# Moving a decode selection into the attention tasks, and cached window keys into the projections, in a one-core hybrid decoder step

## The chip, the cores and the metric

The kernel runs on one NeuronCore of one Trainium2 chip. The metric is device microseconds (us) of one execution, from a median of several runs. Everything is float32. The engines are PE (TensorE; PEld is its weight load), DVE (VectorE), ACT (ScalarE), POOL (GpSimd) and SP (SyncE, which here only starts DMAs). Each engine runs its own list of instructions in order, and semaphores tie the lists together.

## The reference

One layer is applied to a prompt (1 x 512 rows of width 1024) and to a decode group (8 sequences, one new row each, 2048 cached rows in 16 pages each). The part that the change touches is the attention of the decode group:

```python
def nsa_attend(q, gates, qpos, kc, vc, ks, vs, kw, vw, kw_pos):
    s = einsum('bqghd,bngd->bqghn', q, kc) * scale            # compressed branch, 127 blocks
    p = masked_softmax(s, ...)
    o_cmp = einsum('bqghn,bngd->bqghd', p, vc)
    imp = p.sum(axis=3)                                       # importance, summed over the 4 heads of a group
    # score of 33 selection blocks from imp; the first and the last two are forced
    ...
    _, idx = lax.top_k(score, 16)                             # selected branch: 16 of 33 blocks of 64 keys
    s = einsum('bqghd,bqgksd->bqghks', q, k_g) * scale
    o_slc = einsum(..., masked_softmax(s, mask), v_g)
    s = einsum('bqghd,bwgd->bqghw', q, kw) * scale            # window branch: last 512 rows (cached state)
    o_win = einsum('bqghw,bwgd->bqghd', masked_softmax(s, wmask), vw)
    g = sigmoid(gates)
    return g[..., 0:1] * o_cmp + g[..., 1:2] * o_slc + g[..., 2:3] * o_win
```

Around it stand a projection `h @ w_in` (queries, keys and values of three branches, gates, an S5 input), a compression of keys and values by two small layers, an S5 recurrence, a gated merge and an MLP of width 4096. There are 16 heads in 4 groups, the head dimension is 64.

## The kernel before

The whole layer is one program whose order is written out by hand. In time it falls into these stages:

- **Projections** (0 to 302 us). `UNITS` lists them; PE runs one after the other (`projection(u, unit)`), and each writes one of two pairs of PSUM banks (0 to 3), which ACT empties. A "gemm" unit is 16 matmuls of 128 x 260 (L1870); `("tr", c, m)` transposes the tile of keys or values just made; `("y", ii)` are outputs of the S5 recurrence, `("h0",)` and `("st",)` its state in and out. `ENDS_BEHIND` places the four `chunk_ends(ii)` (L1979), that feed the recurrence on DVE, behind units.
- **Key units inside the projections.** The scores of the decode queries against the 2048 cached keys of the selected branch are taken straight from the raw pages. One of 16 units k holds 8 pages of one sequence: SP loads four of them (L706) and POOL gathers four (L872) into one of seven buffers `KL`; DVE transposes the buffer in 32 x 32 blocks into one of two `KT` (L1452); and PE runs 32 matmuls of 32 x 32 by 256 (`key_scores`, L1996) into banks 4 to 7. `KEYS_BEHIND` tells behind which projection unit they stand, some singly and some in twos. Buffer k < 4 is its own, then three go round; `wait_key_buffer` says when one may be filled.
- **Compression** (302 to 453 us). Pages of the compressed cache come through a ring of three slabs (`PLAN`, `SLAB`), DVE permutes them (L1500), PE runs layer 1 (L2041) and layer 2 (L2050, L2052). Scores of the prompt's compressed branch run in between (`compressed_scores`, `compressed_probs` on DVE).
- **Decode selection** (453 to 496 us). Products of the decode queries with the compressed keys (L2071) and the gates (L2073); softmax; importance (L2137); top 16 of 33 by comparing all pairs on 32 partitions (L1612 to L1617); the chosen blocks as a mask added to the 2048 scores `SA` (L1585, L1588), softmax. In the same stage the window branch is scored: `key_t(r)` transposes the cached window keys of one half sequence by four PE transposes, ACT copies them to `XT` (L1103), `key_s` multiplies (L2123); 16 such steps from two slabs `("winrows", (0, bh))`. `head_probs(v)` then transposes ten groups of probabilities (0 to 3 prompt, 4 to 7 selected, 8 window, 9 the rest), in L2091 or L1847, and ACT copies them out (L1144).
- **Attention tasks** (496 to 661 us). 48 tasks `TASKS[n]`, software pipelined: at n, PE runs `scores(n)` (L2153), `probs(n-2)` (transposes, L1847) and `values(n-3)` (L2185, L2190); DVE adds the causal mask (L1657), takes the maximum (L1659), then scales and copies for the tasks before; ACT takes exponentials (L1166). Twelve `decode_values` steps (L2204 to L2215) multiply the decode probabilities with values, at the tasks in `V_AT`: 1, 5, 9, ... 45.
- **Merge and MLP** (661 us to the end), bound by PE (L2277).

Of the kernel before, what the change touches and what calls it, by code (L numbers as in the profile page):

```python
# [6 lines left out]
ALU = mybir.AluOpType  # L7
# [6 lines left out]
P = 128  # L14
# [49 lines left out]
CO_HSUMT = CO_HSUM + 32  # L64
CO_BM = CO_HSUMT + P
# [7 lines left out]
CO_HSUMT2 = CO_PERM + P  # L73
CO_PERMT = CO_HSUMT2 + P
CO_BM2 = CO_PERMT + P
CO_ALL = CO_BM2 + NB


def shape_constants():
# [9 lines left out]
    c[:, CO_HSUM:CO_HSUM + 32] = i[:, None] // HPG == np.arange(32)[None, :]  # L89
    c[:32, CO_HSUMT:CO_HSUMT + P] = i[None, :] // HPG == np.arange(32)[:, None]  # L90
    c[:, CO_BM:CO_BM + NB] = i[:, None] // NH == np.arange(NB)[None, :]
# [8 lines left out]
    c[:32, CO_HSUMT2:CO_HSUMT2 + P] = (NG * (i // HPG % NB) + i // 32)[None, :] == np.arange(32)[:, None]  # L100
    c[:, CO_BM2:CO_BM2 + NB] = i[:, None] // HPG % NB == np.arange(NB)[None, :]
    j = np.arange(NSEL)
    tie = np.broadcast_to((j[None, :] < j[:, None]).astype(np.float32), (32, NSEL, NSEL)).copy()
    return c, tie
# [9 lines left out]
def stream_plan():  # L114
# [9 lines left out]
    plan += [("winrows", (0, bh), 4, 0) for bh in range(2)]  # L124
# [26 lines left out]
def projection_units():  # L151
# [8 lines left out]
            ("y", 2), q_units[2], q_units[3], ("y", 3), ("st",)]  # L160
    prev = None
    for c in range(3):
        for m in range(4):
            rest.append(("gemm", ("win", (C_KV + KVW * c, 512)), m, P, ("kv", c, m)))
            if prev is not None:
                rest.append(("tr", *prev))
            prev = (c, m)
# [10 lines left out]
def label(unit):  # L178
# [12 lines left out]
KEYS_BEHIND = {("kv", 0, 1): (0, 1), ("tr", 0, 1): (2,), ("tr", 0, 2): (3,), ("tr", 0, 3): (4, 5), ("tr", 1, 0): (6,),  # L191
               ("tr", 1, 1): (7,), ("tr", 1, 2): (8, 9), ("tr", 1, 3): (10,), ("tr", 2, 0): (11,),
               ("tr", 2, 1): (12, 13), ("tr", 2, 2): (14,), ("tr", 2, 3): (15,)}
# [3 lines left out]
def build(nc, a):  # L197
    with ExitStack() as ctx:
# [119 lines left out]
        sw_read = sem("sw_read")  # L318
# [4 lines left out]
        xt_full = sem("xt_full")  # L323
        xt_ready = sem("xt_ready")
        xt_used = sem("xt_used")
# [14 lines left out]
        s_full = sem("s_full")  # L340
# [95 lines left out]
        XT = QO[:, 6224:8272].rearrange("p (s c) -> p s c", s=4)  # L436
# [7 lines left out]
        kcT = R[:, 5216:5216 + 8 * 2 * (NC + 2)].rearrange("p (b q n) -> p b q n", b=8, q=2)  # L444
# [3 lines left out]
        SA = QO[:, 4160:6209]  # L448
        SAT = SA[:, 0:2048].rearrange("p (x a t) -> p a x t", a=4, t=32)
        SW = R[:, 13921:14434]  # L450
        SC = R[:, 14434:14563]
        IMP = R[0:32, 14564:14697]
        SSEL = R[0:32, 14700:14733]
        SELX = R[:, 14740:14773]
        GDN = R[:, 14774:14776]
        CMPB = R[0:32, 9824:10913].rearrange("p (j i) -> p j i", j=NSEL)
        CMPA = R[0:32, 10913:12002].rearrange("p (j i) -> p j i", j=NSEL)
        MORE = R[:, 12002:12002 + CO_ALL - CO_N]
        PERM, HSUMT2, PERMT = (MORE[:, c - CO_N:c - CO_N + P] for c in (CO_PERM, CO_HSUMT2, CO_PERMT))
        BM2 = MORE[:, CO_BM2 - CO_N:CO_ALL - CO_N]  # L460
        TIE = R[0:32, 12400:13489].rearrange("p (j i) -> p j i", j=NSEL)
        GH = R[:, 13500:13548]
# [12 lines left out]
        PCF = [R[:, c:c + 512].rearrange("p (h n) -> p h n", n=32) for c in (15968, 16796, 17308, 3072)]  # L475
# [92 lines left out]
        def key_buffer(k):  # L568
            return k if k < 4 else 4 + (k - 4) % 3

        def key_count(k):
            return 64 if k < 4 else 64 * ((k - 4) // 3 + 1)
# [4 lines left out]
        def wait_key_buffer(eng, k):  # L577
# [1798 lines left out]
```

## Time and profile before

| what | value |
|---|---|
| median of 3 runs | 1363.39 us (1362.45 to 1364.57) |
| the profiled execution | 1360.91 us, its span 1359.1 us |
| PE busy | 1251.5 us (92%) |
| DVE busy | 828.9 us (61%) |
| ACT, POOL busy | 305.1 us (22%), 355.7 us (26%) |
| 453.1 to 497.2 us | PE busy 28.4 of 44.1 us, granted clock 0.82 |
| 497.2 to 661 us | PE busy 155.4 and DVE 129.6 of 163.8 us, granted clock 1.00 |

The span runs from the first to the last instruction on the chip; the execution's own time is 1.8 us more. The stretches are read from the view that adds up busy time by window, the rest from the page.

### The profile page before, as it was taken

How to read it: one execution, taken by the hardware profiler on the slowest of the kernel's cores; microseconds unless marked ns; L12 is line 12 of the kernel's file. 1: busy time of each engine (PE TensorE's matmuls, PEld its weight loads, DVE VectorE, ACT ScalarE, POOL GpSimd, SP SyncE). 2: the span in 40 equal slices, each digit the busy share in tenths (PEclk: the TensorE clock that was granted, in tenths of full speed). 3: DMA queues.
4: the chain of work that ended last, by engine and by line, in shares of the span. 5: the costliest groups of instructions: out<-in, count | busy, mean ns of one | idle time of the engine just before them, and what ended most of it. 6: DMA issues, size and time to landing. Idle time of an engine off the chain costs nothing.

```text
span 1359.1 us, 20576 instructions
## 1 busy us (share of the span) xinstructions
PE 1251.5 (92%) x7761; PEld 1017.1 (75%) x7761; DVE 828.9 (61%) x1370; ACT 305.1 (22%) x831; POOL 355.7 (26%) x422
## 2 busy tenths in 40 slices
PE   6889899999999669999999999986999999999995
PEld 5778776668887445565788888775888888888885
DVE  7779332227888477777766554657565465466445
ACT  3463311120010355565410111032000000000012
POOL 5942324312220012222111111110111112513542
PEclk9899899899999889999999999996999999999998
DMA  9223445547667333535561332330122132131101
GB/s 264 72 79 121 148 108 170 160 146 257 242 248 248 105 91 106 162 97 167 178 225 63 109 92 80 140 111 29 62 97 90 63 114 72 62 124 63 63 1 63
DMA packets 122002, 166.15 MB, mean 122 GB/s; under 512 B 36448, under 2 KB 90400, under 8 KB 117552
## 3 DMA queue, kind: packets, MB, share of 16 engines
q1 hardware_dynamic: 103408, 104.72, 24.8%
q0 software_dynamic: 8080, 50.58, 10.5%
q10 hardware_dynamic: 10416, 9.54, 2.1%
q8 instruction: 62, 1.02, 0.3%
q14 instruction: 36, 0.29, 0.1%
HBM read 159.34 MB, written 13.84 MB: 127 GB/s over the span
## 4 chain that ended last, share of the span: by engine, by line
PE 81%; DVE 12%; issue 3%; ACT 3%; POOL 0%; DMA 0%; DVEq 0%; ACTq 0%; PEldq 0%
PE PS L2277 44%; PE PS L1870 13%; PE PS L2041 8%; PE PS L1847 4%; PE PS L1996 2%; PE PS L2185 2%; PE PS L2153 2%; DVE small L1659 2%; PE PS L2215 1%; DVE PS L1657 1%; DVE R L1677 1%; PE PS L1979 1%; PE PS L2020 1%; DVE hT L1259 1%; PE PS L2190 1%
## 5 line engine op out<-in xcount | busy, mean ns | idle before, releaser
L1870 PE MATMUL PS<-hT,stream 128*128 128x260 f32 (+1 forms) x800 | 187.7, 395 | 6.5 <-ACT KVU L1061 4.1
L1870 PEld LDWEIGHTS PS<-hT,stream 128*128 128x128 f32 (+1 forms) x800 | 153.7, 194 | 38.4 <-issue 6.0
L2277 PE MATMUL PS<-R,stream 128*128 128x260 f32 x720 | 168.9, 383 | 2.4 <-PE PS L2277 2.4
L2277 PEld LDWEIGHTS PS<-R,stream 128*128 128x128 f32 x720 | 135.7, 190 | 25.8 <-issue 5.5
L2277 PE MATMUL PS<-R 128*128 128x260 f32 x576 | 134.3, 390 | 3.3 <-DVE R L1822 2.1
L2277 PEld LDWEIGHTS PS<-R 128*128 128x128 f32 x576 | 111.7, 194 | 22.1 <-DVE R L1822 2.5
L2041 PE MATMUL PS<-R 128*128 128x256 f32 (+1 forms) x544 | 121.9, 383 | 5.2 <-DVE R L1500 2.4
L2277 PE MATMUL PS<-R,QO 128*128 128x260 f32 x544 | 123.6, 383 | 1.4 <-DVE QO L1703 1.4
L1777 DVE TENSOR_TENSOR R<-PS,R 128x260 f32<-128x260 f32 x100 | 42.6, 426 | 129.5 <-PE PS L2277 128.8
L2041 PEld LDWEIGHTS PS<-R 128*128 128x128 f32 x544 | 102.1, 197 | 22.1 <-issue 6.1
L2277 PEld LDWEIGHTS PS<-R,QO 128*128 128x128 f32 x544 | 103.3, 190 | 17.6 <-DVE QO L1703 1.8
L1777 DVE TENSOR_TENSOR KVU<-PS,KVU 128x260 f32<-128x260 f32 x92 | 39.1, 426 | 101.3 <-PE PS L2277 90.8
L2277 PE MATMUL PS<-hT,stream 128*128 128x260 f32 x384 | 94.8, 390 | 3.7 <-PE PS L2277 3.0
L1500 DVE STREAM_TRANSPOSE R<-stream 128x2048 f32<-128x2048 f32 (+1 forms) x34 | 75.2, 2233 | 20.5 <-PE PS L1996 9.8
L2277 PEld LDWEIGHTS PS<-hT,stream 128*128 128x128 f32 x384 | 73.1, 193 | 18.7 <-issue 6.8
L1452 DVE STREAM_TRANSPOSE R<-R 128x2048 f32<-128x2048 f32 x14 | 32.0, 2302 | 86.7 <-PE PS L1996 86.1
L872 POOL DMA_INDIRECT R<-in_cache_kv_slc,row_kv x56 | 53.4, 953 | 117.3 <-DVE R L1452 53.2
L1211 ACT ACTIVATE R<-PS 128x260 f32<-128x260 f32 x56 | 21.5, 386 | 273.9 <-PE PS L2277 273.9
L645 POOL TENSOR_SCALAR R<-R,small 128x512 f32<-128x512 f32 (+3 forms) x64 | 48.1, 755 | 132.8 <-DVE small L1664 132.8
L1847 PEld LDWEIGHTS PS<-consts,R 128*128 128x128 f32 (+1 forms) x424 | 47.6, 145 | 41.5 <-issue 34.1
L1847 PE MATMUL PS<-consts,R 128*128 128x128 f32 (+1 forms) x424 | 61.2, 286 | 13.3 <-DVE R L1677 6.2
L1166 ACT ACTIVATE R<-PS,small 128x512 f32<-128x512 f32 (+3 forms) x128 | 65.9, 525 | 10.9 <-DVE small L1659 10.0
(420 smaller groups left out, 1931.2 us busy)
## 6 DMA issues: line engine op xcount, KB each, us to landing
stream<-in_cache_kv_slc SPq DMA_DIRECT2D x128, 128.0 KB
stream<-in_w_mlp_up SPq DMA_DIRECT2D x8, 2048.0 KB
stream<-in_w_mlp_down SPq DMA_DIRECT2D x8, 2048.0 KB
stream<-in_w_in SPq DMA_DIRECT2D x4, 2048.0 KB
stream<-in_state_kv_win SPq DMA_DIRECT2D x16, 512.0 KB
stream<-in_w_in SPq DMA_DIRECT2D x8, 1024.0 KB
out_kv_win_sample<-in_state_kv_win POOLq DMA_DIRECT2D x1, 8176.0 KB, 43.3
R<-in_cache_kv_slc SPq DMA_DIRECT2D x56, 128.0 KB
```

The costliest lines, as they stand in the source:

```text
L645: return eng.tensor_scalar(S, S, ainv[:, k:k + 1], gtm[:, t, col:col + 1], ALU.mult, ALU.mult)
L872: pool.indirect_dma_start(key_pages(k)[:, x, :], None, slc_rows, bass.IndirectOffsetOnAxis(ap=row_kv[:, at:at + 1], axis=0)).then_inc(keys ...
L1166: ins = nc.scalar.activation(PP[:, n % 2, j, c0:c0 + P * (t + 1)], score_block(n, j, c0), ACT.Exp, bias=amx[:, k:k + 1], accum_out=asm[:, ...
L1452: V.transpose(KT[k % 2], KL[key_buffer(k)]).then_inc(kt_ready, 1)
L1500: V.transpose(ROWST[:, w % 3, 0:256 * ns].rearrange("p (s x) -> p s x", x=256), slab(s)[:, 0:512 * ns].rearrange("p (s k x) -> p k s x", k ...
L1659: V.reduce_max(amx[:, k:k + 2 * nx], S[:, :, 0:P * (t + 1)], AX, negate=True).then_inc(as_max, 1)
L1777: V.tensor_tensor(to, product_of(w, i), other, ALU.add).then_inc(pr_added, 1)
L1847: return nc.tensor.transpose(out, in_, ident[0:rows, 0:rows])
L1870: ins = M(pair(u)[0:w, hf, 0:HALF], lhs[k], rhs[k][:, HALF * hf:HALF * hf + HALF], start=(k == 0), stop=(k == n - 1))
L1996: ins = M(PS[32 * g:32 * g + 32, 4 + a4, cols], QM[rows, 256 * b + c0:256 * b + c0 + 32], keys[rows, :, c0:c0 + 32], start=(k == 0 and dh ...
L2041: ins = M(out, w1c[:, kind, x, :], rhs, start=(x == 0), stop=(x == 7))
L2277: ins = M(product_of(w, i), lhs[:, k, :], rhs[:, k, :], start=(k == 0), stop=(k == nk - 1))
```

## The change

- **The window keys become four key units** of the projections (`NWU = 4`, two sequences each, 64 matmuls of 32 x 32 by 128), ahead of the sixteen page units. Their scores `SW` are copied out once by ACT behind `("tr", 0, 2)`. `key_t`, `key_s`, `XT` and the two `("winrows", (0, bh))` slabs go.
- **One key unit at a time**: ten stand between the two halves of a gemm unit (`KEYS_INSIDE`), ten behind a transpose unit (`KEYS_BEHIND`). Page loads use buffers 2 to 6 in turn at first, then 4 to 6. SP takes pages 0 to 3 of a unit and POOL 4 to 7 (before: even and odd ones), SP reads four page numbers by one load, and the compression weights come in four parts between page loads.
- **Two units move**: `("st",)` from behind `("y", 3)` to behind the first gemm unit of keys; `chunk_ends(0)` from behind `("h0",)` to behind `("q", 7)`.
- **The selection moves into the tasks**: DVE's steps stand behind tasks 0 to 9 (`selection(n)`), PE's behind 1 and 4 (`selection_products(n)`), and groups 8, 4, 5, 6, 7, 9 of the probabilities behind 8, 10, 11, 12, 13, 14 (`PROBS_AT`), all through bank 4. The pair comparison runs on 128 partitions over 297 elements, not on 32 over 1089. Only groups 0 to 3 stand ahead of the tasks. The `decode_values` steps stand at 15, 16, 18, 21, 24, 27, 30, 31, 33, 36, 40, 44.
- The gates' product (L2073) moves into the compression stage, and one `compressed_probs` of two moves from step 6 to step 5.

```diff
-ENDS_BEHIND = [("h0",), ("q", 4), ("y", 0), ("y", 1)]
+ENDS_BEHIND = [("q", 7), ("q", 4), ("y", 0), ("y", 1)]
...
-NKU = 2 * NB
-KEYS_BEHIND = {("kv", 0, 1): (0, 1), ("tr", 0, 1): (2,), ("tr", 0, 2): (3,), ("tr", 0, 3): (4, 5), ("tr", 1, 0): (6,),
...
+NWU = NB // 2
+NKU = NWU + 2 * NB
+KEYS_INSIDE = {("kv", 0, 1): 0, ("kv", 0, 2): 2, ("kv", 1, 0): 4, ("kv", 1, 1): 6, ("kv", 1, 2): 8, ("kv", 1, 3): 10,
+               ("kv", 2, 0): 12, ("kv", 2, 1): 14, ("kv", 2, 2): 16, ("kv", 2, 3): 18}
+KEYS_BEHIND = {("tr", 0, 0): 1, ("tr", 0, 1): 3, ("tr", 0, 3): 5, ("tr", 1, 0): 7, ("tr", 1, 1): 9, ("tr", 1, 2): 11,
+               ("tr", 1, 3): 13, ("tr", 2, 0): 15, ("tr", 2, 1): 17, ("tr", 2, 2): 19}
+KEY_BUFFER = [0, 1, 2, 3, 4, 5, 6, 2, 3] + [4 + k % 3 for k in range(NKU - 9)]
...
+            elif k < 12:
+                eng.wait_ge(kt_ready, (3, 4, 5, 6, 7)[k - 7])
             else:
                 eng.wait_ge(kt_ready, k - 2)
...
-        PT_BANK = (0, 1, 2, 3, 5, 6, 7, 5, 6, 7)
+        PT_BANK = (5, 6, 7, 5, 4, 4, 4, 4, 4, 4)
...
+        N_PC, N_IMP, N_SEL, N_SELX, N_MASK, N_SWE, N_SAE, N_SWP, N_SAP = 0, 1, 3, 4, 5, 6, 8, 7, 9
+        PROBS_AT = {8: 8, 10: 4, 11: 5, 12: 6, 13: 7, 14: 9}
+        PT_ORDER = [0, 1, 2, 3] + list(PROBS_AT.values())
...
-        V_AT = {1 + 4 * i: step for i, step in enumerate(V_STEPS)}
+        V_AT = dict(zip((15, 16, 18, 21, 24, 27, 30, 31, 33, 36, 40, 44), V_STEPS))
...
-                        key_loads(4, 5, 6)
-                        compression_weights()
-                        key_loads(7, 8, 9)
+                        key_loads(*range(4, 12))
+                        sp.wait_ge(kt_ready, 9)
+                        for q in range(3):
+                            compression_weights(q)
+                            key_loads(12 + q)
...
+            def selection(n):
+                if n == N_PC:
+                    dve.wait_ge(sc_exp, 1)
...
+                if n == N_SEL:
+                    Si = SSEL.unsqueeze(1).to_broadcast([P, JQ, NSEL])
+                    Sj = SJ[:, 0].unsqueeze(2).to_broadcast([P, JQ, NSEL])
...
+                if n == N_MASK + 1:
+                    selected(0)
+                    selected(1)
+                if n == N_MASK + 2:
+                    selected(2)
+                    selected(3)
+                    V.reduce_max(dmx[:, 1:2], pmx, AX, negate=True).then_inc(samax, 1)
+                if n == N_SWP:
+                    dve.wait_ge(sexp, 1)
...
+                if n == N_SAP:
+                    dve.wait_ge(saexp, 1)
...
+            pe.wait_ge(pcp_ready, TT)
+            for v in range(4):
+                head_probs(v)
+            scores(0)
             pe.wait_ge(pt_ready, 4)
-            scores(0)
-            pe.wait_ge(pa_ready, 1)
-            for v in range(4, 8):
-                head_probs(v)
-            pe.wait_ge(p_ready, 1)
-            head_probs(8)
-            head_probs(9)
-            pe.wait_ge(pt_ready, 10)
             for n in range(NTK + 3):
...
+                selection_products(n)
+                if n in PROBS_AT:
+                    head_probs(PROBS_AT[n])
+                if n == min(V_AT):
+                    pe.wait_ge(pt_ready, 10)
                 if n in V_AT:
                     decode_values(*V_AT[n])
```

In the program's order the change looks as follows. First PE in the projections, before, behind the last S5 output unit: `L1847 ... small` is the unit `st`, L1870 a gemm unit, L1996 a key unit.

```order
L1847 MATMUL PS<-consts,small 128x128 [waits h_ready,hs_ready,pair_free]
L1847 MATMUL PS<-consts,small 16x128
L1847 MATMUL PS<-consts,small 128x128
L1847 MATMUL PS<-consts,small 16x128
L1870 MATMUL PS<-hT,stream 128x260 [waits slab_in0,pair_free]
L1870 MATMUL PS<-hT,stream 128x260 x15
L1870 MATMUL PS<-hT,stream 128x260 [waits slab_in0,pair_free]
L1870 MATMUL PS<-hT,stream 128x260 x15
L1996 MATMUL PS<-R 32x256 [waits kt_ready,ends_free,qm_ready]
L1996 MATMUL PS<-R 32x256 x31
L1996 MATMUL PS<-R 32x256 [waits kt_ready]
L1996 MATMUL PS<-R 32x256 x31
```

The same place after (L1886 was L1847, L1911 was L1870, L2042 is a window key unit):

```order
L1911 MATMUL PS<-hT,stream 128x260 [waits slab_in0,pair_free]
L1911 MATMUL PS<-hT,stream 128x260 x15
L1886 MATMUL PS<-consts,small 128x128 [waits h_ready,hs_ready,pair_free]
L1886 MATMUL PS<-consts,small 16x128
L1886 MATMUL PS<-consts,small 128x128
L1886 MATMUL PS<-consts,small 16x128
L1911 MATMUL PS<-hT,stream 128x260 [waits slab_in0,pair_free]
L1911 MATMUL PS<-hT,stream 128x260 x7
L2042 MATMUL PS<-R 32x128 [waits kt_ready,ends_free,qm_ready]
L2042 MATMUL PS<-R 32x128 x63
L1911 MATMUL PS<-hT,stream 128x260 x8
L1886 MATMUL PS<-consts,QO 128x128 [waits pair_free]
```

The unit `st` stands between two gemm units instead of ahead of them, and a window unit of 64 matmuls splits the second one.

Then PE between the products with the compressed keys (L2071) and the first tasks, before. The list starts at the decode masks' products; the window key steps stand ahead of it:

```order
L2153 MATMUL PS<-KVU,QO 128x512 [waits pt_ready]
L2153 MATMUL PS<-KVU,QO 128x512
L2091 MATMUL PS<-R,QO 128x128 [waits pt_ready,pa_ready]
L2091 MATMUL PS<-R,QO 128x128 x3
L2091 MATMUL PS<-R,QO 128x128 [waits pt_ready]
L2091 MATMUL PS<-R,QO 128x128 x3
L2091 MATMUL PS<-R,QO 128x128 [waits pt_ready]
L2091 MATMUL PS<-R,QO 128x128 x3
L2091 MATMUL PS<-R,QO 128x128 [waits pt_ready]
L2091 MATMUL PS<-R,QO 128x128 x3
L1847 MATMUL PS<-consts,R 128x128 [waits pt_ready,p_ready]
L1847 MATMUL PS<-consts,R 128x128 x3
```

After, from the products with the compressed keys (L2124) on; L2173 is `scores`, L2159 the importance, L2205 and L2210 `values`:

```order
L2124 MATMUL PS<-QO,R 32x129 [waits l2_ready,qpad_ready]
L2124 MATMUL PS<-QO,R 32x129 x15
L1886 MATMUL PS<-consts,QO 128x128 [waits pcp_ready]
L1886 MATMUL PS<-consts,QO 128x128 x11
L1886 MATMUL PS<-consts,QO 128x128 [waits pt_ready]
L1886 MATMUL PS<-consts,QO 128x128 x3
L2173 MATMUL PS<-KVU,QO 128x512 x2
L2173 MATMUL PS<-KVU,QO 128x512 [waits pt_ready]
L2173 MATMUL PS<-KVU,QO 128x512
L2159 MATMUL PS<-R,consts 128x127 [waits pc_ready]
L2173 MATMUL PS<-KVU,QO 128x128 [waits as_exp]
L2173 MATMUL PS<-KVU,QO 128x128 x3
```

Between these products and `scores(1)` only the prompt's sixteen transposes are left; the sixteen matmuls of L2091 with their wait on `pa_ready` are gone from here.

Last DVE in the tasks 2 to 4 after (L1695 mask and L1697 maximum begin a task, L1715 ends its own work); before, nothing stood between an L1677 copy and the next mask:

```order
L1715 COPY R<-PS 128x512 [waits at_full]
L1640 TENSOR_TENSOR R<-R 128x297 [waits tie_in]
L1641 TENSOR_TENSOR R<-R 128x297
L1642 TENSOR_TENSOR R<-R 128x297 [waits dve_ch]
L1643 TENSOR_TENSOR R<-R 128x297 [waits dve_ch]
L1644 TENSOR_REDUCE R<-R 128x9 [waits dve_ch]
L1647 TENSOR_SCALAR R<-R 32x9 [waits dve_ch]
L1647 TENSOR_SCALAR R<-R 32x9 x2
L1647 TENSOR_SCALAR R<-R 32x6
L1695 TENSOR_TENSOR PS<-PS,consts 128x2x128 [waits as_full]
L1697 TENSOR_REDUCE small<-PS 128x2 [waits as_mask]
```

The comparison of pairs now stands between the copy of one task and the mask of the next.

## Rows read from the trace of the kernel before

**Rows 1.** The page: instruction fetches among the DMA queues; the chain's shares

```profile
q8 instruction: 62, 1.02, 0.3%
...
PE 81%; DVE 12%; issue 3%; ACT 3%; POOL 0%; DMA 0%; DVEq 0%; ACTq 0%; PEldq 0%
```

**Rows 2.** Chain of waits, 450 to 498 us: start, length, engine, tile, line

```profile
453.14 0.59 PE PS L2073 x2
...
478.24 0.70 DVE QO L1585
...
484.22 2.10 ACT QO L1135 x2
...
486.74 1.30 DVE QO L1634
...
488.54 5.83 PE PS L2091 x32
...
497.22 0.44 DVE PS L1657
```

**Rows 3.** Timeline, 450 to 500 us: start, length, engine, line, operation [idle before]

```profile
456.12 1.28 ACT L1130 ACT_TABLE_LOAD   x1
...
461.12 1.28 DVE L1612 TENSOR_TENSOR R<-R 32x1089 f32<-32x1089 f32 x1
...
488.39 0.16 DVE L1639 RECIPROCAL small<-small 128x1 f32<-128x1 f32 x1
...
490.57 1.22 DVE L1659 TENSOR_REDUCE small<-PS 128x2 f32<-128x1024 f32 x1
490.65 0.60 ACT L1144 ACTIVATE R<-PS 128x512 f32<-128x512 f32 x1 [3.64 <-PE PS L2091]
```

**Rows 4.** Windows of the tasks: PE, PEld, DVE, ACT, POOL busy, clock, DMA

```profile
497.22:526.98 29.76, 27.37 (x293) 17.00 (x287) 23.97 (x48) 18.27 (x64) 9.02 (x12) 1.00 0.25 72
526.98:543.62 16.64, 16.14 (x164) 10.33 (x164) 13.35 (x26) 9.34 (x30) 5.02 (x6) 1.00 0.41 120
543.62:661.00 117.38, 111.83 (x1150) 71.41 (x1152) 92.32 (x184) 69.68 (x232) 34.73 (x48) 1.00 0.47 141
```

**Rows 5.** Timeline of PE in the tasks

```profile
509.73 1.92 PE L2215 MATMUL PS<-stream,R 128*16 128x256 f32 x32
...
518.49 1.09 PE L1847 MATMUL PS<-consts,R 128*128 128x128 f32 x8
```

**Rows 6.** Timeline of PE in the projections

```profile
156.54 16.79 PE L1870 MATMUL PS<-hT,stream 128*128 128x260 f32 x64 [4.13 <-ACT KVU L1061]
173.25 2.76 PE L1996 MATMUL PS<-R 32*32 32x256 f32 x128
...
176.55 7.18 PE L1870 MATMUL PS<-hT,stream 128*128 128x260 f32 x32
...
213.67 0.73 PE L1996 MATMUL PS<-R 32*32 32x256 f32 x26
...
220.07 8.74 PE L1870 MATMUL PS<-hT,stream 128*128 128x260 f32 x32
...
249.26 0.69 PE L1996 MATMUL PS<-R 32*32 32x256 f32 x26
...
255.66 9.71 PE L1870 MATMUL PS<-hT,stream 128*128 128x260 f32 x32
```

**Rows 7.** Windows in the projections, the columns as in rows 4

```profile
157.00:162.00 5.00, 5.00 (x14) 3.88 (x14) 3.25 (x2) 0.25 (x2) 3.79 (x4) 0.54 0.86 269
```

**Rows 8.** Timeline of PE around the first chunk ends

```profile
80.04 3.59 PE L1979 MATMUL PS<-QO,R 128*128 128x136 f32 x16 [3.72 <-issue]
```

**Rows 9.** Timeline of ACT in the same stretch

```profile
79.63 0.60 ACT L1010 ACTIVATE QO<-PS 128x520 f32<-128x520 f32 x1
```

**Rows 10.** Timeline of POOL: one gather of a page

```profile
224.11 0.95 POOL L872 DMA_INDIRECT R<-in_cache_kv_slc,row_kv  x1 [0.30 <-issue]
```

**Rows 11.** Timeline of PE in the compression stage

```profile
428.43 7.17 PE L2041 MATMUL PS<-R 128*128 128x256 f32 x32 [2.36 <-DVE R L1500]
```

More of the change, by code:

```diff
@@ L166, in projection_units @@
                 rest.append(("tr", *prev))
+            if prev is None:
+                rest.append(("st",))
             prev = (c, m)
@@ L568, in key_buffer, with key_landed @@
         def key_buffer(k):
-            return k if k < 4 else 4 + (k - 4) % 3
-        def key_count(k):
-            return 64 if k < 4 else 64 * ((k - 4) // 3 + 1)
+            return KEY_BUFFER[k]
+        def key_landed(k, windows, pages):
+            mine = [i for i in range(k + 1) if KEY_BUFFER[i] == KEY_BUFFER[k]]
+            return 16 * sum(windows if i < NWU else pages for i in mine)
         def key_pages(k):
@@ L1031, in _ @@
                     nkv += 1
+                    if (c, m) == (0, 2):
+                        act.wait_ge(k_done, NWU)
+                        for a4 in range(4):
+                            ins = nc.scalar.activation(SWT[:, a4], PS[:, 4 + a4, 0:P].rearrange("p (x t) -> p x t", t=32),
+                                                       ACT.Copy)
+                        ins.then_inc(sw_ready, 1)
                     continue
@@ L1863, in open_pair, with gemm @@
                     pe.wait_ge(pair_free, u - 1)
-            def gemm(u, lhs, rhs, w=P):
+            def gemm(u, lhs, rhs, w=P, inside=None):
                 n = len(lhs)
                 for hf in range(2):
+                    if hf == 1 and inside is not None:
+                        key_scores(inside)
                     for k in range(n):
@@ L1905, in projection @@
                     S = slab(n)[:, 0:KD * width].rearrange("p (k c) -> p k c", c=width)
-                    ins = gemm(u, [S[:, k, P * m:P * m + w] for k in range(KD)], [hT[:, k, :] for k in range(KD)], w)
+                    ins = gemm(u, [S[:, k, P * m:P * m + w] for k in range(KD)], [hT[:, k, :] for k in range(KD)], w,
+                               KEYS_INSIDE.get(unit[4]))
                     ins.then_inc(pair_full, 1)
@@ L2014, in compressed_products @@
                     pe.wait_ge(sa_ready, 1)
+                    M(PS[:, 4, 136:184], consts[0:NB, CO_BMT:CO_BMT + P], gs8[0:NB, :], start=True,
+                      stop=True).then_inc(gates_full, 1)
                 else:
@@ L2116, in key_s @@
-            def key_s(r0):
-                pe.wait_ge(xt_ready, r0 + 4)
-                if r0 == 0:
-                    pe.wait_ge(sc_max, 1)
-                for r in range(r0, r0 + 4):
-                    b, p = KR[r]
-                    jj, bh = b // 2, b % 2
-                    M(PS[32 * jj:32 * jj + 32, 4, :], QP[:, p, b, :], XT[:, r % 4, :],
-                      start=(bh == 0 and p == 0), stop=(bh == 1 and p == 1)).then_inc(xt_used, 1)
-                if r0 == 12:
-                    pe.wait_ge(xt_used, 16)
-                    pe.sem_inc(s_full, 1)
@@ L2129, in _, with selection_products @@
-            for r in range(len(KR) + 1):
-                if r < len(KR):
-                    key_t(r)
-                if r % 4 == 1 and r >= 5 or r == len(KR):
-                    key_s((r - 1) // 4 * 4 - (4 if r < len(KR) else 0))
-                if r == R_IMP:
+            def selection_products(n):
+                if n == N_IMP:
                     pe.wait_ge(pc_ready, 1)
-                    M(PS[0:32, 5, 0:NC], consts[:, CO_HSUM:CO_HSUM + 32], SC[:, 0:NC], start=True,
+                    M(PS[:, 4, 192:192 + NC], consts[:, CO_HSUM:CO_HSUM + P], SC[:, 0:NC], start=True,
```

381 lines of the change are left out of this document (187 added, 194 removed).

## The prediction

> **What bounds the kernel now.** I read the chain of waits first: PE holds 81% of it and DVE 12% [rows 1], so a microsecond counts where PE's list waits, not where an engine merely has work. Then I walked the chain through the decode selection. The products with the compressed keys end at 453.14 [rows 2], and the first mask of the steady tasks starts at 497.22 [rows 2]. In between the chain runs over DVE masks and maxima, one exponential of 2049 columns on ACT, a scaling, and transposes [rows 2]: 44.1 us of serial steps with PE used in part only.
>
> The tasks behind it are different. By the windows, PE is busy for 27.37 of the first 29.76 us, DVE for 23.97 [rows 4]; over the rest PE for 111.83 of 117.38 and DVE for 92.32 [rows 4]. PE sets the pace, DVE has a fifth to spare. Added DVE work is therefore half hidden there, added PE work hardly.
>
> In the projections PE runs matmul after matmul, with three disturbances. PE waits 4.13 us for ACT, and the two gemm units behind it take 16.79 us [rows 6] where one takes 7.18 [rows 6]; the granted clock over those 5 us is 0.54 [rows 7], a mean between the two levels (1.2 and 2.4 GHz), after an idle stretch. And two key units stop in their middle: they start at 213.67 and 249.26 and are followed by the next gemm unit at 220.07 and 255.66 [rows 6]; the gemm units behind take 8.74 and 9.71 us. In both stops PE waits for nothing that the profile names.
>
> **Ahead of the tasks.** What goes: the whole way from 453.14 to 497.22, 44.1 us. What stays, from the same start: two small DVE steps of about 0.3 each (between the 0.16 of one element and the 0.70 of 512 columns [rows 2, 3]), 0.6; the table load 1.28 [rows 3] and a 127-column exponential, 0.5; the first copy 0.60 [rows 3], since the fourth group of transposes shares its bank; that group's four transposes and `scores(0)`, 1.09 each [rows 5]; mask and maximum of task 0, 0.44 + 1.22 [rows 2, 3]; the first step of the selection, 0.65. Sum 7.5, and the mask of task 1 starts there. Gain 44.1 - 7.5 = **-36.6**.
>
> **Inside the tasks, DVE.** The selection's DVE steps do not vanish; now they queue between one task's copy and the next task's mask, and PE's `scores` and `values` wait behind. By rows: eight 512-column steps (four mask adds, four maxima) at 0.72, the 0.70 [rows 2] and a gap, 5.8 and the window's maximum 0.7; the scaling of 2049 columns 1.30 [rows 2]; the window's scaling 0.5; the comparison, five steps of 297 elements. One of 1089 took 1.28 [rows 3]; on a line from 0.16 for one element that is 0.47, so 2.35 instead of 6.4. Some thirty small steps at 0.16 to 0.3 [rows 3] make 4.5. Total 15.2, of which 14.5 lies in tasks 1 to 9. Before, that stretch lasted 29.76 with 23.97 on DVE [rows 4]; after, DVE alone needs 23.97 + 14.5 = 38.5, and I take 39.3 with its semaphore steps: +9.5. PE's small products (importance, mask, window group) then lie under DVE.
>
> **Inside the tasks, PE.** Groups 4 to 7 and 9 of the probabilities stand behind tasks 10 to 14: four at 1.09 [rows 5] and 0.6, 5.0 on the engine that paces. Before, that stretch held PE for 16.14 of 16.64 [rows 4] with one value step of 1.92 [rows 5], now moved later. 16.1 - 1.9 + 5.0 = 19.2; about 0.5 of waits: +3. Here the wait for `pa_ready` (DVE, behind task 9) holds `scores(11)`, and DVE has 2.9 us of its own work meanwhile, so I add 1 for all such handovers. The value steps: four more fall behind task 15, where PE paces (an `own` step of 1.5 and three of 1.92 [rows 5]): 7.3, of which the 5.5 idle us of PE there [rows 4] may take a little: +6.5. Tasks together **+20** (15 to 28).
>
> **Projections.** (1) `st` behind the first key gemm: ACT empties the last S5 unit while PE multiplies. The wait 4.13 goes, and the slow gemms with it: 16.79 - 2 x 7.18 = 2.43 [rows 6]; a new wait of 0.3 for the first key tile's copy. -6.3. (2) `chunk_ends(0)` behind `q 7`: PE was idle 3.72 us before it [rows 8]. But `q 7` needs the bank pair of `q 6`, and ACT empties that only at 79.63 + 0.60 [rows 9], behind its chunk copies. The idle time stays; DVE gets its input some 4 us later and had over 10 to spare. 0 (to -1.9). (3) Four window units. Two page units (128 records of 32 x 256) took 2.76 [rows 6]. A window unit has 128 records of half the columns. If the issue of instructions sets the rate, it costs 2.76; if the columns do, 1.38. A 32 x 256 record at sixteen at once would be far below the 22 ns that each took, so issue is nearer: +11.0 (5.5 to 11.0). The sixteen page units cost what they did.
>
> The Trainium skill, TensorEngine Tiling (Array Packing), section Key Properties, says that different tiles load weights and multiply in parallel; by that alone the columns would count, and the sum would be 5.5 lower. No row has a 32 x 128 form.
>
> (4) The two stops. From start to the next gemm 6.40 each time [rows 6] where a unit takes 1.4, so 5.0 each, and 1.56 + 2.53 in the slow gemms behind: 14.1 in all. Both came in the first unit behind two in a row, with page loads under way. In the new order no two stand together, but a window unit is as many instructions as two page units, and more bytes move early. I keep 8 of the 14.1: -6 (-14 to +14). Projections together **-1.3**.
>
> The Trainium skill, Runtime: NRT & Kernel Launch, section Instruction fetch mechanics, says that instructions come in 16 KiB blocks and that this is mostly hidden. The block size agrees with 62 packets for 1.02 MB [rows 1]; that it is hidden doesn't agree with the stops, if they are fetches, which no row proves.
>
> **Compression.** PE waited 2.36 us for a DVE transpose [rows 11] behind the two `compressed_probs` in one step; spread, that goes. The gates' product, 0.59 [rows 2], is now there. **-1.8** (-2.4 to 0). SP loads two slabs fewer.
>
> **Sum.** -36.6 + 20 - 1.3 - 1.8 = -19.7. The profiled execution took 1360.9 us, so 1341.2; the median is 2.5 higher, 1363.4, and by it **1344**.
>
> **Rivals.** *More is gained*: the stops go altogether (-8 more) and a window unit costs its columns (-5.5): 1344 - 13.5 = 1330. For it: no two units together. Against: the record rate of [rows 6].
>
> *The chain moves into the tasks*: DVE's steps of one task become the wait of PE, whose wait delays the next mask, and PE, idle for 3 us at a time, falls to the lower clock as at [rows 7]. Price: PE's work in tasks 1 to 9, 27.4, at a mean clock of 0.75 (estimated between 0.54 [rows 7] and 1), +9, and 3 of handovers: 1356. Against it: DVE never waits for a result younger than one task.
>
> *Slower, PE stops in the projections*: window units fetch as many instructions in 2.76 us as the pairs did, and five page buffers plus the window rows keep the queues full. A stop costs 14.1 / 2 = 7 us. The forecast holds about one; it takes 19.7 / 7, three more, to eat the gain, so it decides from the fourth. With six, 1344 + 35 = 1379. For it: both stops of before; against: fourteen other units passed.
>
> *The pages come too late*, so the fixed order buys nothing: POOL's gather takes 0.95 + 0.30 [rows 10], four a unit are 5.0 us, and PE asks for a unit each (7.18 + 0.7 + 2.8) / 2 = 5.3. Covered by 0.3 only. At 6.3 a unit, eleven units behind the five buffers wait 1 us each: 1355.
>
> **How the numbers follow.** The forecast has 0.66, with its own range 1334 to 1354 from the bounds above; more gained 0.13; chain in the tasks 0.10; pages late 0.04; slower 0.07. The range takes in the first rival's edge and the middle ones: 1331 to 1359. A measurement of this kernel tells 0.2%, about 2.7 us, from no change. Faster by more: all but the last case and a tail, 0.90; within 0.03; slower 0.07.
>
> **What would show it.** Right: the mask of task 1 about 8 us behind the end of the products with the compressed keys; DVE over 90% busy in tasks 1 to 9; each task with a probability group about 1 us longer; window units of 2.8 us; no wait for ACT ahead of the second key gemm; a granted clock near 1 from the products to the last task. Wrong: PE waits without a named cause in more than two key units; PE waits for `kt_ready`; a clock under 0.9 in the tasks; value steps that wait for DMA, since SP now has them closer together.

## The result, and the profile after

The changed kernel took **1383.9 us** (median of 4 runs, 1383.3 to 1389.0) beside 1362.9 (4 runs, 1357.8 to 1364.6) for the kernel before: a ratio of 1.0176 with a 95% interval of 1.0156 to 1.0196. It is slower by 21 us where 19 us faster was forecast. That is the case with the chance 0.07, the rival "PE stops in the projections".

The chain of waits of the changed kernel, at its landmarks (start us, length us, what). The rows answer to [rows 2] and [rows 6].

```profile
152.05 7.01 PE PS L1911 x32
...
348.81 3.31 PE PS L2094 x14
...
494.61 1.95 PE PS L2124 x32
...
503.01 0.44 DVE PS L1695
...
687.47 2.61 PE PS L1911 x11
```

They are the first key gemm, the start of the compression, the end of the products with the compressed keys (at 496.56), the mask of task 1 and the gemm behind the tasks. Beside those of before, stage by stage:

| stage | before | after | difference | forecast |
|---|---|---|---|---|
| start to the compression | 302.5 | 348.8 | +46.3 | -1.3 |
| compression to the end of its products | 150.7 | 147.8 | -2.9 | -1.8 |
| products to the mask of task 1 | 44.1 | 6.4 | -37.6 | -36.6 |
| tasks, from that mask to the next gemm | 164.1 | 184.5 | +20.4 | +20 |
| the rest | 697.8 | 694.0 | -3.8 | 0 |
| span | 1359.1 | 1381.5 | +22.4 | -19.7 |

Four stages came within 4 us of what was forecast. One did not, and it outweighs them. What happened in it stands on the chain, here from the first window unit on:

```profile
164.60 0.38 PE PS L2042 x16
164.98 0.15 issue
165.13 0.26 PE PS L2042
165.39 1.86 issue
167.25 0.26 PE PS L2042
167.51 1.18 issue
168.69 0.37 PE PS L2042
169.05 1.03 issue
170.09 2.67 PE PS L2042 x105
172.76 4.56 PE PS L1911 x16
```

"issue" is time in which PE waits for nothing that the profile names. The trace holds two records for each matmul, so a window unit has 128 records and a page unit 64. PE runs 16 records, then one at a time, 0.4 to 2.1 us from one to the next, then the others without a pause, 25 ns each. The half gemm behind takes 4.56 us instead of 3.7, with a granted clock of 0.81 over it. The same is seen, to more or less of it, in twelve more units. The next lines are page unit 5, which stops, and units 6 and 7, which do not:

```profile
221.22 1.24 PE PS L2047 x41
...
222.53 0.38 PE PS L2047
222.91 1.04 issue
223.95 0.62 PE PS L2047 x3
224.57 0.81 issue
225.38 1.12 PE PS L2047 x18
226.50 4.99 PE PS L1911 x16
231.49 1.43 PE PS L2047 x60
...
237.16 1.43 PE PS L2047 x60
```

POOL's own row of instructions (start us, us) says what else went on at 221 to 224. Behind 223.45 its next gather is at 241.31:

```profile
219.69 0.95 POOL L887 DMA_INDIRECT R<-in_cache_kv_slc,row_kv  x1 [8.39 <-DVE R L1465]
...
223.45 0.95 POOL L887 DMA_INDIRECT R<-in_cache_kv_slc,row_kv  x1 [0.30 <-issue]
241.31 0.95 POOL L887 DMA_INDIRECT R<-in_cache_kv_slc,row_kv  x1 [16.91 <-DVE R L1465]
```

Units 4, 6, 7 and 16 to 18 ran clean; these are the units beside which no page load is under way. Unit 19 stands beside two gathers of the compression (333.05 and 334.30) and took 3.1 us, with two short pauses, where unit 18 took 1.5. But SP's loads, POOL's gathers and DVE's transposes all come together, each started by the transpose of an earlier unit. The trace alone can't tell which of them stops PE, or whether so many short instructions in a row do it by themselves. One thing it does tell. Over the stop of the first window unit, 164.90 to 170.10 us, the queues moved this (packets, MB, share of 16 engines):

```profile
q0 software_dynamic: 197, 0.52, 37.2%
q10 hardware_dynamic: 176, 0.15, 8.3%
q1 hardware_dynamic: 83, 0.07, 5.5%
```

No packet of instructions is among them, and none in the stops at 262.80 to 265.90 and 281.30 to 284.40 either. So what ends these three is not the arrival of a block of instructions.

### The profile page after: what moved, and what is told of

Its sections match the earlier page's. It is cut to its first block, busy times and chain, and to the rows that moved or that the text cites. A ratio compares the mean times of both kernels' runs of the same rounds, so it can differ in the third digit from the quotient of the medians.

```text
span 1381.5 us, 21274 instructions
## 1 busy us (share of the span) xinstructions
PE 1276.5 (92%) x8182; PEld 1027.1 (74%) x8182; DVE 835.8 (61%) x1382; ACT 297.0 (22%) x819; POOL 355.4 (26%) x422
## 3 DMA queue, kind: packets, MB, share of 16 engines
q8 instruction: 65, 1.06, 0.3%
## 4 chain that ended last, share of the span: by engine, by line
PE 84%; DVE 9%; issue 4%; ACT 2%; POOL 0%; DMA 0%; DVEq 0%; ACTq 0%; PEldq 0%; POOLq 0%
PE PS L2298 43%; PE PS L1911 15%; PE PS L2094 8%; PE PS L1886 4%; PE PS L2047 3%; PE PS L2173 2%; PE PS L2205 2%; DVE small L1697 1%; PE PS L2235 1%; PE PS L2042 1%; PE PS L1976 1%; DVE PS L1695 1%; DVE R L1514 1%; DVE R L1715 1%; PE PS L2073 1%
## 5 line engine op out<-in xcount | busy, mean ns | idle before, releaser
L1911 PE MATMUL PS<-hT,stream 128*128 128x260 f32 (+1 forms) x800 | 201.2, 412 | 6.8 <-ACT QO L1026 4.0
L1911 PEld LDWEIGHTS PS<-hT,stream 128*128 128x128 f32 (+1 forms) x800 | 159.7, 203 | 45.7 <-issue 10.5
L2298 PEld LDWEIGHTS PS<-R,stream 128*128 128x128 f32 x720 | 135.7, 190 | 25.8 <-issue 5.5
L2298 PE MATMUL PS<-R 128*128 128x260 f32 x576 | 130.8, 383 | 3.3 <-DVE R L1861 2.1
L2298 PEld LDWEIGHTS PS<-R 128*128 128x128 f32 x576 | 109.3, 190 | 21.1 <-DVE R L1861 2.5
L2094 PEld LDWEIGHTS PS<-R 128*128 128x128 f32 x544 | 100.8, 194 | 20.2 <-issue 5.4
L1465 DVE STREAM_TRANSPOSE R<-R 128x2048 f32<-128x2048 f32 x18 | 41.6, 2311 | 122.1 <-PE PS L2047 85.4
L887 POOL DMA_INDIRECT R<-in_cache_kv_slc,row_kv x64 | 60.9, 952 | 175.9 <-DVE R L1465 82.2
L1886 PEld LDWEIGHTS PS<-consts,R 128*128 128x128 f32 (+1 forms) x403 | 45.8, 146 | 40.5 <-issue 35.0
L1886 PE MATMUL PS<-consts,R 128*128 128x128 f32 (+1 forms) x403 | 59.1, 289 | 13.2 <-POOL R L650 6.9
```

The lines of the kernel that those rows point to most:

```text
L887: pool.indirect_dma_start(key_pages(k)[:, x, :], None, slc_rows, bass.IndirectOffsetOnAxis(ap=row_kv[:, at:at + 1], axis=0)).then_inc(keys ...
L1465: V.transpose(KT[k % 2], KL[key_buffer(k)]).then_inc(kt_ready, 1)
L1886: return nc.tensor.transpose(out, in_, ident[0:rows, 0:rows])
L1911: ins = M(pair(u)[0:w, hf, 0:HALF], lhs[k], rhs[k][:, HALF * hf:HALF * hf + HALF], start=(k == 0), stop=(k == n - 1))
L2094: ins = M(out, w1c[:, kind, x, :], rhs, start=(x == 0), stop=(x == 7))
L2298: ins = M(product_of(w, i), lhs[:, k, :], rhs[:, k, :], start=(k == 0), stop=(k == nk - 1))
```

## Experiments

Every experiment has runs of the kernel before beside it, on the same chip: e1 to e4 on chip A, e5 and e7 to e9 on B, e10 to e13 on C, e14 and e16 to e18 on D, e15 and e19 on C again. The chip of the result above is not known, and no experiment ran the changed kernel as it is on A or B.

**Which loads.** Three kernels leave out page loads behind unit 6. PE's instructions stay the same.

```diff
-            for k in range(NWU, NKU):
+            for k in range(NWU, 7):
                 wait_key_buffer(pool, k)
...
-                for k in units:
+                for k in [k for k in units if k < 7]:
                     wait_key_buffer(sp, k)
```

The first piece alone is e2, the second alone e3, both are e1. DVE's waits count accordingly.

> The changed kernel without the page loads of key units 7 to 19, SP's and POOL's both; these units multiply what lies in their buffers. PE's instructions, their order and the transposes stay. Theory (page traffic): PE's stops inside key units come from the page loads that are under way; without them units 7 to 19 take 2.8 to 3.2 us each, PE's time from 151.9 to the compression falls from 197 to about 160, and the time from 1384 to about 1347. Rival (instructions): the units' own 256 instructions cannot be supplied at this rate whatever the queues do; then the stops stay, and the time is 1384 less at most 5.

> The changed kernel without POOL's half of the page loads (the gathers) of units 7 to 19; SP's half stays. If POOL's gathers are what stops PE, the time is about 1347, as without any page load. If any traffic does it, in proportion, about half of the gain: 1365. If SP's loads do it, 1384.

> The changed kernel without SP's half of the page loads of units 7 to 19; POOL's gathers stay. If POOL's gathers are what stops PE, about 1384; in proportion to traffic 1365; if SP's loads do it, 1347.

Measured, with the kernel before at 1359.8: e1 1336.4 (2 runs), e2 **1336.9** (2 runs), e3 **1382.2** (2 runs, 1379.7 to 1384.7). Where 1347 was expected, 10 us less came; which theory holds doesn't hang on that. Beside the 1383.9 of the result, SP's half costs nothing that two runs can tell, and POOL's half costs all of it. The groups of PE between 150 and 350 us (busy, mean ns, idle time before them), first of the changed kernel, then of e2, then of e3:

```profile
L1911 PE MATMUL PS<-hT,stream 128*128 128x260 f32 (+1 forms) x416 | 110.5, 426 | 1.3 <-issue 1.3
L2047 PE MATMUL PS<-R 32*32 32x256 f32 x1024 | 41.6, 395 | 10.4 <-issue 9.2
L2042 PE MATMUL PS<-R 32*32 32x128 f32 x512 | 14.4, 350 | 9.1 <-issue 8.9
```

```profile
L1913 PE MATMUL PS<-hT,stream 128*128 128x260 f32 (+1 forms) x416 | 98.3, 391 | 0.3 <-issue 0.3
L2049 PE MATMUL PS<-R 32*32 32x256 f32 x1024 | 25.3, 385 | 0.5 <-DVE R L1467 0.4
L2044 PE MATMUL PS<-R 32*32 32x128 f32 x512 | 10.4, 306 | 4.4 <-issue 4.4
```

```profile
L2049 PE MATMUL PS<-R 32*32 32x256 f32 x1024 | 43.3, 387 | 7.2 <-issue 5.6
L2044 PE MATMUL PS<-R 32*32 32x128 f32 x512 | 15.1, 339 | 8.8 <-issue 8.7
```

The page units fell from 52.0 us with their idle time to 25.8, and the gemms from 110.5 to 98.3, though SP kept loading. Over 164 to 300 us the DMA share was 0.44 in e2, which has next to no stops, and 0.33 in e3, which has nearly all of them (0.48 in the changed kernel). So traffic as such is no cause. The 4.4 us left in e2 lie in the first window unit alone, beside the last of the twelve gathers that e2 keeps; its other three window units have no pause.

**Where the units stand.** The units are the same, but two at a time behind the transposes:

```diff
+KEYS_INSIDE = {}
...
-                    key_scores(KEYS_BEHIND[label(unit)])
+                    key_scores(KEYS_BEHIND[label(unit)] - 1)
+                    key_scores(KEYS_BEHIND[label(unit)])
```

> The changed kernel, complete, with the key units in pairs behind the transposes instead of one inside a gemm and one behind: the same instructions, loads and buffers. Theory (page traffic): what counts is which unit stands beside a burst of loads; in pairs, a burst is started by two transposes at once and lasts longer, one unit in two may escape: 1365 to 1390. Rival (position): a unit inside a gemm is what stops, since the gemm's accumulation is cut in two; then the ten inside units lose their stops and the time falls to about 1360.

1352.9 (8 runs), ratio 0.9957 (0.9941 to 0.9972) to the kernel before. Both theories missed: beside the 1383.9 of the result, this one feature of the change costs 31 us where gathers hurt. The trace gives the reason. A burst of four gathers takes 4.7 us and starts behind a transpose. Behind a pair stands a whole gemm, 7.2 us, and the burst often falls beside it; the pairs at 206.8, 217.3 and 286.8 ran clean, each behind the end of a burst. With a unit after every half gemm, 3.7 us apart, nearly every burst meets a unit.

**Which property of the gathers.** In the next four the list of PE stays as it was; e5 and e7 give POOL's loads to SP, e8 and e9 replace them on POOL.

> The changed kernel, complete, with all eight page loads of a key unit issued by SP and none gathered by POOL. Theory (POOL's gathers stop PE): the same bytes move, yet the stops go: 1337 plus what DVE waits for SP, which issues eight loads a unit (0.55 each, 4.4 of 5.3 us) and the compression's weights beside them, 0 to 10 us: 1337 to 1347, faster than before by 1 to 1.7%. Rival (half the traffic was enough to remove the stops, from whichever side): the doubled load on SP's queue stops PE in its turn, above 1365.

> The kernel before, complete, with all eight page loads of a key unit issued by SP and none gathered. If the two stops of before (14.1 us with the slow gemms behind) were the same thing, they go: 1346 to 1350. If they had another cause (two units in a row), they stay: 1360, or more where DVE waits for SP.

> The changed kernel with POOL filling its half of each page unit's pages with zeros (four memsets of 256 columns) where it gathered them: the waits and their order stay, the gathered keys are left out of the result. If it is the gathers' transfer (their queue) that stops PE, the time is about 1337, as without gathers. If it is POOL being at work between the units, about 1384.

> The changed kernel, complete, with POOL's four gathers of a unit replaced by four direct loads of the same pages by POOL, their address from a register. If it is a transfer issued by POOL that stops PE (its software queue), about 1384 as with gathers. If it is the gather with its list of 128 row numbers, 1337 to 1347.

The edit of e9:

```diff
-                    pool.indirect_dma_start(key_pages(k)[:, x, :], None, slc_rows, bass.IndirectOffsetOnAxis(
-                        ap=row_kv[:, at:at + 1], axis=0)).then_inc(keys_pool[key_buffer(k)], 16)
+                    v = pool.value_load(pages[0:1, at:at + 1], min_val=0, max_val=N_PHYS - 1)
+                    pool.dma_start(key_pages(k)[:, x, :], a["cache_kv_slc"].rearrange("n t k g d -> n t (k g d)")
+                                   [bass.DynSlice(v, 1)].rearrange("o t c -> (o t) c")[:, 0:256]
+                                   ).then_inc(keys_pool[key_buffer(k)], 16)
```

Measured beside 1361.7 (14 runs) for the kernel before: e5 1346.8 (5 runs), e7 1366.0 (10), e8 1327.8 (2), e9 **1326.1** (2; ratio 0.9752, 0.9707 to 0.9797). All but e8 compute everything. e8 and e9 came out some 10 us below what was expected, and e7 (1346 to 1350 expected) missed by 16. In e8 POOL fills memory between the units, 318 ns for each page instead of 952, and no page or window unit stops but the last: POOL at work, for a third of the time, does not do it. In e9 the same queue moves the same bytes, as the rows of the queues show for the changed kernel and then for e9 (packets, MB, share of 16 engines):

```profile
q0 software_dynamic: 8080, 50.58, 10.4%
```

```profile
q0 software_dynamic: 8080, 50.58, 10.8%
```

Only the instruction differs, and with it the time it holds POOL (0.54 us instead of 0.95). PE's groups in e9, 150 to 310 us, have almost no "issue" left:

```profile
L1913 PE MATMUL PS<-hT,stream 128*128 128x260 f32 (+1 forms) x416 | 97.1, 388 | 0.3 <-ACT QO L1028 0.3
L2049 PE MATMUL PS<-R 32*32 32x256 f32 x1024 | 25.3, 385 | 1.5 <-DVE R L1467 1.1
L2044 PE MATMUL PS<-R 32*32 32x128 f32 x512 | 7.6, 278 | 0.0
```

The units do stand beside direct loads: the one at 231.68 runs clean between loads that start at 230.82, 231.96 and 233.10. Two things in the same trace show that gathers do hurt on this chip. The last page unit (276.65) still takes 3.0 us with two pauses, beside gathers of the compression at 276.21 and 277.56, which e9 keeps. And the group of 128 x 1 products behind it, beside two more, has 0.7 us of "issue", as it has (0.7 or 0.8) in every kernel on A and B and in the two of the result, and in none on C and D; first e9, then the changed kernel on D:

```profile
L2008 PE MATMUL PS<-R 128*64 128x1 f32 x64 | 2.4, 198 | 1.0 <-issue 0.7 <-PE PS L1913 0.3
```

```profile
L2006 PE MATMUL PS<-R 128*64 128x1 f32 x64 | 2.0, 197 | 0.3 <-PE PS L1911 0.3
```

So it is the gather, an indirect transfer with 128 row numbers, that stops PE, on this chip. e5 and e7 have no stops in their key units either (but for the short one beside the compression's gathers), but they trade them for a queue that is too slow. The row of e5:

```profile
L2039 PE MATMUL PS<-R 32*32 32x256 f32 x1024 | 27.9, 422 | 17.6 <-DVE R L1457 17.2
```

PE waits 17.2 us for transposes, and those wait for SP. I had allowed 0 to 10. In e7 the same wait is 15.9 us, and its compression starts at 307.7, 5.2 us later than the 302.5 of the kernel before in the trace of the result: 1366.0 against 1361.7.

**Is it the kernel alone?** The next four ran on chip C.

> The kernel before, complete, with POOL's four gathers of a key unit replaced by four direct loads of the same pages from the same queue, as in e9. Theory (the gathers stop PE, in before too): its two stops and the slow gemms behind them go, 14.1 us: 1346 to 1350. Rival (the stops of before came from two units in a row or from traffic): 1360 to 1364. If the theory holds, the difference to e9 is what the change gains by its own design: 1348 - 1326 = 22, against 19.7 forecast.

> The kernel of e9 once more, word for word, beside the others of this call, for an interval: 1325 to 1328.

> The kernel of e9 with the key units in pairs behind the transposes, as in e4. If where a unit stands matters only through the gathers, 1325 to 1329, no difference to e9. If a pair asks for its second transpose sooner than DVE has it (2.3 us beside a unit of 2.8), PE waits up to 0.5 in ten places: 1331.

> The changed kernel, complete, with two of POOL's four loads of a unit still gathered and two direct. If the cost goes by the number of gathers, half of 58 us is left: 1355. If a unit stops at any gather beside it, 1375 to 1384. If only a burst of four back to back does it, 1326 to 1335.

e11 took 1326.5 (4 runs) again, e10 1340.5 (10 runs). But the kernel before itself took **1338.8** (13 runs, 1336.9 to 1342.9) where it had taken 1360 to 1363 on three other occasions. The ratio of e10 to it is 1.0006 (0.9994 to 1.0019). On this chip the kernel before had nothing to lose, so the question put to e10 isn't answered, and e13 (1331.2, 2 runs) can't be read as a dose. e12 took 1331.9 (4 runs, 1325.0 to 1334.5): the pairs cost 5 us without any page gather. Its trace shows 4.4 us of waits for DVE, and two single stops of 1.7 and 1.3 us, 3.0 together, in the second window unit of each pair, 256 records in a row. These are of another kind: each is one pause and not many, and a packet of instructions lands 1.3 to 1.4 us ahead of its end (170.8 and 172.1; 184.7 and 186.1). That fits a row of short instructions too long for their supply, at a price of 3 us; no run isolates it.

> The changed kernel itself, unchanged. In the call with e10 the kernel before took 1338.8 on its chip where it had taken 1360 to 1364, and so gained nothing from direct loads; e9 and e11 took 1326 on both. Open is whether the changed kernel, too, takes another time there. Theory (what a gather costs PE differs from chip to chip): on a chip where the kernel before takes 1339, this takes 1327 to 1340; on one where it takes 1362, 1384. Rival (the changed kernel's stops are its own, on every chip): 1384 on both.

> The kernel before itself, for its trace on this chip. Where it takes 1339, the two stops and the slow gemms behind them (14.1 us), and 8 us more in places not yet named, are gone from the key units; where it takes 1362, they are there as on record.

> The kernel before with direct loads by POOL, word for word e10, since e10 fell on a chip where the kernel before had nothing to lose. On a chip where the kernel before takes 1362: 1340 if the gathers are what costs it 22 us there, 1362 if not. On one where it takes 1339: 1340 again.

> The changed kernel with each of POOL's four gathers of a unit cut to 32 of its 128 rows; the other rows are not loaded. The number of gathers is the same, the rows a quarter. On a chip where the changed kernel takes 1384: 1384 if the cost goes by gathers, 1340 if it goes by rows or by their transfer. Where the changed kernel takes under 1340, it tells nothing and should take the same.

Chip D is again one on which the kernel before takes 1339.6 (13 runs). There the changed kernel, unaltered, took **1327.5** (4 runs, 1323.7 to 1330.5): ratio 0.9925 (0.9906 to 0.9944). The same program is 1.8% slower than before on one chip and 0.75% faster on another. e18 took 1338.6 (10 runs) and e14 1327.1 (2 runs), as the theory has it. PE's groups of e16, 60 to 350 us, with all 64 gathers in place:

```profile
L2047 PE MATMUL PS<-R 32*32 32x256 f32 x1024 | 25.3, 385 | 0.0
L2042 PE MATMUL PS<-R 32*32 32x128 f32 x512 | 8.9, 278 | 0.0
```

It isn't that the units escape the bursts there. Thirteen of the twenty units of e16 begin inside a burst of gathers (the one at 216.34, say, in the burst from 215.35 to 220.05), and none of them pauses. A gather holds POOL as long on both (a median of 949 ns in the trace of the result, 946 in e16); what it does to PE differs. Why, no run shows. Of the four chips gathers hurt on two, A and B, each seen once, and don't on C and D; C was seen twice, with the same time for the kernel before (1338.8 and 1339.0). That it is the chip fits this and isn't more than likely, since the runs on A and B were also the earlier ones.

> The kernel of e9 (changed, direct loads) with the transposes of the S5 states back ahead of the first key gemm, as in the kernel before. The prediction priced that move at 6.3 us (4.1 of PE waiting for ACT, 2.4 of slow gemms, less 0.3): 1332 against 1326. If the wait only moved elsewhere: 1326. Direct loads give the same time on every chip so far, so this can be read on any.

> The kernel of e14 once more, since e14 ran on a chip where whole gathers cost nothing: 32 of the 128 rows in each of the four gathers, the rest not loaded. On a chip where the kernel before takes 1360 to 1364 (and the changed one 1384): 1384 if the cost goes by the number of gathers, about 1340 if by rows. On one where it takes 1339: 1327, and the question stays open.

e15 took 1333.1 (10 runs) against 1326.5 of e11 on the same chip: the move is worth 6.6 us, forecast 6.3. The wait is back on the chain and in the group of gemms:

```profile
L1911 PE MATMUL PS<-hT,stream 128*128 128x260 f32 x672 | 160.0, 396 | 8.4 <-ACT KVU L1083 4.1 <-ACT QO L1026 4.0 <-ACT R L1061 0.2
```

e19 took 1325.6 (2 runs), but with the kernel before at 1339.0: whether the cost goes by gathers or by rows stays open.

## Why the prediction was wrong

**The step that failed** is (4) of the projections: "I keep 8 of the 14.1: -6 (-14 to +14)". Against a chip without stops (e16, e17), the compression started 17.3 us later in the kernel before (302.5 against 285.2) and 58.1 later in the changed one (348.8 against 290.7). The stops, with the slow gemms behind them, grew by 41 us. The term was +41, far outside its own range. Its cause, two units in a row or too many instructions, was wrong as well: the page gathers stop PE (e2, e3, e9), and with every unit alone they stopped thirteen. I had seen both stops of before, had noted page loads under way and two units in a row, and took the second as the likelier cause, since fourteen units passed. The right question was what those fourteen lacked. In the trace of before, POOL's bursts of gathers answer it: two bursts of eight (207.7 to 217.4 and 243.0 to 252.7) lie beside the two stops, and each of the others ends before the next unit starts, by 0.3 to 6.3 us. Of the fourteen that "passed" one did not quite: the unit at 285.81 took 2.9 us, beside a gather of the compression at 285.36, and in e17 it took 1.6. From there one asks where the bursts fall in the new order: a transpose starts one, and the next unit comes one half gemm, 3.7 us, behind, inside the 4.7 us of the burst. Thirteen of the twenty units stand so. At the 7 us of a stop of before that is 91, at the 4.5 us that they turned out to cost (58.1 / 13) it is 58. My rival of six stops at 7 us came out near the measured time (1379), with a chance of 0.07 against 0.66, and that was luck: it had the place right, but it took the fetch of instructions and full queues for the cause, and thirteen stops of 4.5 us came where it had six of 7. Two of the signs named for a wrong forecast came: PE waits without a named cause in more than two key units (thirteen, and a short one), and a clock under 0.9 in the tasks (0.80).

**The rest of the sum held to a few microseconds.** By e16 and e17, on one chip and without stops, the landmarks are these; first the kernel before (start of the compression, the gates' product, mask of task 1, gemm behind the tasks):

```profile
285.23 6.42 PE PS L2041 x32
...
435.89 0.59 PE PS L2073 x2
...
478.88 0.44 DVE PS L1657
...
644.17 5.90 PE PS L1870 x26
```

and the changed one:

```profile
290.70 3.85 PE PS L2094 x32
...
434.98 1.95 PE PS L2124 x32
...
443.44 0.45 DVE PS L1695
...
627.89 12.25 PE PS L1911 x55
```

- Ahead of the tasks: 43.0 to 6.5 us, -36.5 (forecast -36.6).
- Tasks: +19.2 by these two (forecast 20). By parts against [rows 4] two errors cancel. Masks 1 to 10 take 42.4 instead of 29.8, +12.7, where I had +9.5. DVE's work was right, 38.0 against 38.5, but the granted clock there is 0.80 (the first row below), not near 1, and PE needs 33.3 us where it needed 27.4. The lower clock is what the rival "chain moves into the tasks" had foreseen (0.75); it cost 3 us beyond the forecast, not the rival's 12. Tasks 10 to 14 cost +2.1 instead of +4, the rest +5.7 instead of +6.5. The windows of the changed kernel on record, masks 1 to 10 and 10 to 15 (length; PE, PEld, DVE, ACT, POOL busy; clock; DMA share, GB/s):

```profile
503.01:545.43 42.42, 33.32 (x244) 23.53 (x244) 38.01 (x89) 22.60 (x73) 9.05 (x12) 0.80 0.03 9
545.43:564.12 18.69, 17.76 (x152) 12.35 (x147) 13.43 (x27) 11.63 (x37) 5.08 (x6) 1.00 0.00 1
```

- Compression: -2.9 on record, -4.4 here (forecast -1.8).
- Window units: 512 records in 8.9 us without stops, 2.2 a unit, between the two ends of 5.5 and 11.0; I took 11.0. (Without gathers beside them they take 7.6: e8, e9.) The reason given for 11.0 was a misreading: I held that a 32 x 256 record, sixteen at once, would be far below 22 ns, but one lasts 385 ns in the trace, a sixteenth of which is 24. The sixteen page units, forecast to cost what they did, went from 23.1 to 25.3 us (e17, e16), so that the two errors cancel. The projections without the stops come to +5.5, where terms (1) and (3) gave +4.7.
- `st`: right, by e15. `chunk_ends(0)`: right, worth nothing; PE's idle stretch there is 3.99 us (up to 80.32), where it was 3.72.
- The rest, forecast as no change, got 3.5 to 3.8 us shorter; the cause stays open.

Together that is -19.8 by two profiled executions and about -12 by the medians (1327.5 against 1339.6), the profile of e17 being at the top of its kernel's runs and that of e16 at the bottom of its own. So the agreement of 19.8 with the forecast of 19.7 is luck, and stage differences between these two traces hold to a few microseconds only. The stop term of -6 was not to be had there, since before has no stops; without it the sum is -13.7, 2 us from the medians. For such a chip the other terms are right in mechanism.

**A version that is fast on both kinds of chip** is e9: 1326.1 on B and 1326.5 on C, whatever the kernel before does there (1361.7 and 1338.8). On a chip without stops it is no faster than the changed kernel (1327.5 on D). The change is good; what it needs is direct loads.

## What to carry over

When an engine stops without a named cause, list what ran beside the stop and what did not run beside the cases that passed; a cause that explains only the stops is half of one. Keep indirect gathers away from stretches in which PE runs hundreds of short matmuls, or load the pages directly with the page number in a register, on the same queue: that cost nothing, and where gathers hurt it took 58 us out (1383.9 to 1326.1). And before a forecast rests on a stop, ask whether it belongs to the kernel: a difference of 2% may have another sign on the next chip.

## What the hardware did that I had not expected

- Indirect gathers of 128 rows stopped PE's 32-row matmuls on chips A and B and in the runs of the result, not on C and D. Where they do, a stop starts 16 to 46 records into a unit of the changed kernel, lets one or a few through per 0.3 to 2 us, and ends 1 to 2 us after the last gather of the burst does: at 225.38 behind the gather that ends at 224.40, at 170.09 behind 167.85. The compression's gathers did it too, to the last page unit (3.1 us instead of 1.6 in e16) and to 128 x 1 products (3.2 instead of 2.0), but not to matmul records of 380 ns: 380 ns in the changed kernel, 380 in e9, 376 in e16.
- The Trainium skill, Runtime: NRT & Kernel Launch, section Instruction fetch mechanics, has fetches in 16 KiB blocks as mostly hidden. The traces agree in number and size: 65 packets, 1.06 MB, with stops and without. Three of the long stops have no such packet in them and end before the next one comes (that of 164.98 to 170.09 before the one at 172.83), so a late block is not what ends them; what holds PE stays open. The two pauses of e12 do have one.
- A 32 x 128 record took 15 ns without gathers beside it and 17 with them (7.6 us for 512 in e9, 8.9 in e16), a 32 x 256 one 25 (25.3 us for 1024): twice the columns cost half to two thirds as much again. The prediction had drawn from the Trainium skill, TensorEngine Tiling (Array Packing), section Key Properties, that the columns would count; the rows put the price between the two ends.
- POOL starts a direct load of 128 rows in 0.54 us, a gather of as many in 0.95 (groups of e9 and of the changed kernel).
